# Last combination of a two-layer decoder step: normalisation moments of the odd token tiles on ScalarE, identity products and one square root at the stage's start

## The reference, cut to what matters

```python
def layer_norm(x, g, b, eps=LN_EPS):
    mu = xf.mean(-1, keepdims=True)
    var = jnp.square(xf - mu).mean(-1, keepdims=True)
    return ((xf - mu) * lax.rsqrt(var + eps) * g + b)
...
    y = y + dense_gate[:, e:e + 1] * (h @ w_down[e])
...
x = layer_norm(ALPHA * x + f, prm['ln_ffn_g'][layer], prm['ln_ffn_b'][layer])
```

## Time and profile before

| | us |
|---|---|
| median of 3 runs | 1498.75 |
| lowest, highest | 1495.86, 1498.77 |
| the profiled execution, its device time | 1502.35 |
| span of the profiled execution | 1500.5 |
| start of the last combination in it | about 1446.4 |
| end of the last VectorE instruction | about 1496.9 |
| TensorE busy, VectorE busy, ScalarE busy over the span | 92%, 49%, 29% |

### The profile page before, as it was taken

The page is one execution under the profiler, slowest core; times in us unless marked ns, Lnnn a source line. Parts: engine busy times, 40 slices in busy tenths (PEclk is TensorE's granted clock), DMA queues, the critical chain, the costliest instruction groups (busy, mean ns, idle before and its releaser), DMA issues. The chain is left out here.

```text
span 1500.5 us, 28132 instructions
## 1 busy us (share of the span) xinstructions
PE 1374.4 (92%) x11029; PEld 806.2 (54%) x11030; DVE 737.1 (49%) x1095; ACT 442.4 (29%) x804; POOL 227.3 (15%) x257
## 2 busy tenths in 40 slices
PE   6999999999689998999978999994998899999956
PEld 5666666666578886454554333331797633333322
DVE  1004444368357762677573334333795634343328
ACT  1003445542233332111113333332232133333311
POOL 4000000000333432110001111113300111111131
PEclk8999999999789998999999999997899999999978
DMA  8492000000210012100347787884503797877445
GB/s 222 85 375 91 22 29 29 29 1 0 60 37 4 4 33 78 62 29 28 122 184 294 281 309 297 328 267 141 188 1 116 269 338 262 330 285 281 155 173 208
DMA packets 73898, 226.76 MB, mean 151 GB/s; under 512 B 21970, under 2 KB 35267, under 8 KB 61226
## 3 DMA queue, kind: packets, MB, share of 16 engines
q1 hardware_dynamic: 52994, 151.13, 29.9%
q0 software_dynamic: 15184, 53.67, 10.0%
q10 hardware_dynamic: 5616, 20.45, 3.4%
HBM read 176.42 MB, written 50.35 MB: 151 GB/s over the span
## 5 line engine op out<-in xcount | busy, mean ns | idle before, releaser
L2445 PE MATMUL ex_pb<-ew_w_gate_up,ex_xT 128*64 x624 | 279.5, 601 | 5.7 <-DVE x_rows L2659 3.8
L2446 PE MATMUL ex_pb<-x_rows,ex_xT 128*64 128x512 f32 x624 | 279.5, 601 | 0.0
L517 PE MATMUL pj_pb<-pj_xT,pj_w 128*128 128x348 f32 (+1 forms) x912 | 275.5, 458 | 0.6 <-ACT pj_xT L552 0.6
L517 PEld LDWEIGHTS pj_pb<-pj_xT,pj_w 128*128 128x128 f32 x912 | 170.1, 189 | 94.5 <-issue 5.7
L2445 PEld LDWEIGHTS ex_pb<-ew_w_gate_up,ex_xT 128*64 128x64 f32 x624 | 83.0, 138 | 170.7 <-issue 170.7
L2659 DVE COPY x_rows<-ew_w_gate_up 128x2048 f32 x80 | 98.0, 1225 | 123.2 <-PE ex_pb L2446 111.7
L2430 PE MATMUL ex_pb<-ew_w_down,ex_hiddenT 128*64 x312 | 145.3, 609 | 4.7 <-ACT ex_hiddenT L2526 4.7
L2431 PE MATMUL ex_pb<-x_rows,ex_hiddenT 128*64 128x512 f32 x312 | 145.3, 609 | 0.0
L2510 ACT COPY x_rows<-ew_w_down 128x2048 f32 x39 | 74.1, 1899 | 117.5 <-PE ex_pb L2431 117.5
L2430 PEld LDWEIGHTS ex_pb<-ew_w_down,ex_hiddenT 128*64 128x64 f32 x312 | 40.3, 139 | 80.4 <-issue 80.4
L2446 PEld LDWEIGHTS ex_pb<-x_rows,ex_xT 128*64 128x64 f32 x624 | 83.0, 138 | 0.0
(11 more groups left out here) (430 smaller groups left out, 2242.7 us busy)
## 6 DMA issues: line engine op xcount, KB each, us to landing
ew_w_gate_up<-in_w_ex_gate_up SPq DMA_DIRECT2D x64, 1024.0 KB, 7.2
ew_w_down<-in_w_ex_down_by_row SPq DMA_DIRECT2D x32, 1024.0 KB, 9.2
scratch_slots_out<-ex_y_rows ACTq DMA_DIRECT2D x39, 512.0 KB
scratch_slots_out<-pj_tmp POOLq DMA_DIRECT2D x3, 4096.0 KB, 21.7
scratch_x_stored<-x_rows SPq DMA_DIRECT2D x16, 512.0 KB
pj_w<-in_w_in SPq DMA_DIRECT2D x7, 1024.0 KB, 9.3
minus_kk_then_y<-in_x_prompt SPq DMA_DIRECT2D x8, 512.0 KB, 5.5
mo_x_in<-in_x_prompt SPq DMA_DIRECT2D x8, 512.0 KB, 3.5
```

The lines of the kernel that those rows point to most:

```text
L517: last = nc.tensor.matmul(product(at)[:, 0:tn], w[:, k_slab % NW, k, c0:c0 + mrows], xT[:, k, x0:x0 + tn], start=(k == 0), stop=(k == KD - 1))
L2445: mm(pb[0:HALF, 2 + u, :], xT[:, k, 0:HALF], w[:, k, :], start=(k == 0), stop=(k == KD - 1))
L2446: last = mm(pb[HALF:P, 2 + u, :], xT[:, k, HALF:P], half_wgu[:, k, :], start=(k == 0), stop=(k == KD - 1))
```

## The change

A square root of `eps` that nobody reads (`eps_root`) is put on ScalarE after the first four diagonals. TensorE starts the stage with `keep_busy` of 28 products into bank 7, before its wait for the gathered rows of tile 0. For odd tiles (1, 3, 5, 7) ScalarE takes the moments: a pass Identity over the tile with a running sum; the sum times -1/D; a pass Square with the negated mean as bias and a running sum; and the root of the second sum over D plus eps. The results of both passes are written over `expert_rows` of that tile, and are not read. VectorE then does only centre, reciprocal and finish for odd tiles; its centre waits for the sum of squares. Even tiles are handled as before. The new helper bodies replace `norm_stats`, `norm_centre`, `norm_root` and `norm_finish` in this stage only.

```diff
+        moments = m.sb("moments", [P, 2, 5])
+        eps_root = m.sb("eps_root", [P, 1])
...
         @block.tensor
         def _(pe):
+            keep_busy(nc, pb[:, 7, :], const["ident"], 28)
             for i in range(TILES):
...
+            def moments_of(i):
+
+                n, o = rows(i), i // 2
+                seen = r[0:n, i, 0, :]
+                total, minus_mean, squares, root = (moments[0:n, o % 2, k:k + 1] for k in range(4))
+                act.wait_ge(q["res"], i + 1)
+                nc.scalar.activation(seen, summed(i), ACT.Identity, accum_out=total).then_inc(q["sum"], 1)
+                act.wait_ge(q["sum"], o + 1)
+                if o >= 2:
+                    act.wait_ge(q["g"], i - 3)
+                nc.scalar.activation(minus_mean, total, ACT.Identity, scale=-1.0 / D).then_inc(q["mean"], 1)
+                act.wait_ge(q["mean"], o + 1)
+                nc.scalar.activation(seen, summed(i), ACT.Square, bias=minus_mean, accum_out=squares).then_inc(q["squares"], 1)
+                act.wait_ge(q["squares"], o + 1)
+                if o >= 2:
+                    act.wait_ge(q["rs"], i - 3)
+                nc.scalar.activation(root, squares, ACT.Sqrt, bias=eps[0:n, :], scale=1.0 / D).then_inc(q["root"], 1)
...
             act.wait_ge(q["eps"], 1)
+            nc.scalar.activation(eps_root[:, :], eps[:, :], ACT.Sqrt)
             for i in range(TILES):
-                norm_root(nc, act, q, i, rows(i), st, eps)
+                if i % 2:
+                    moments_of(i)
+                else:
+                    root_of(i)
                 if i + 2 < TILES:
                     diagonals(i + 2)
...
             for i in range(TILES):
-                norm_stats(nc, dve, q, i, summed(i), st)
-                norm_centre(nc, dve, q, i, x_(i), summed(i), st, g)
-                norm_finish(nc, dve, q, i, x_(i), st, b)
+                n = rows(i)
+                if i % 2:
+                    shift, root, rs = (moments[0:n, i // 2 % 2, k:k + 1] for k in (1, 3, 4))
+                    dve.wait_ge(q["squares"], i // 2 + 1)
+                    stt(out=x_(i), in0=summed(i), scalar=shift, in1=g[0:n, :], op0=ALU.add, op1=ALU.mult).then_inc(q["g"], 1)
+                else:
+                    mean, root, rs = (st[0:n, i // 2 % 2, k:k + 1] for k in (12, 14, 15))
+                    stats(i)
+                    stt(out=x_(i), in0=summed(i), scalar=mean, in1=g[0:n, :], op0=ALU.subtract, op1=ALU.mult).then_inc(q["g"], 1)
```

More of the change, by code:

```diff
@@ L2698, in combine @@
         st = m.sb("stats", [P, 2, 18])
+        moments = m.sb("moments", [P, 2, 5])
+        eps_root = m.sb("eps_root", [P, 1])
         eps = m.sb("eps", [P, 1])
         pb = m.psum("pb", [P, 8, 512])
-        q = {k: m.sem(k) for k in "eps diag res st var root rs g x out".split()}
+        q = {k: m.sem(k) for k in "eps diag res st var sum mean squares root rs g x out".split()}
         s_r = [m.sem(f"rows{i}") for i in range(TILES)]
@@ L2753, in diagonals, with root_of @@
                                          scale=gates[0:n, i, c:c + 1]).then_inc(q["diag"], 1)
+            def moments_of(i):
[14 more added lines that the diff above has]
+                nc.scalar.activation(root, squares, ACT.Sqrt, bias=eps[0:n, :], scale=1.0 / D).then_inc(q["root"], 1)
+            def root_of(i):
+                n, e = rows(i), i // 2
+                act.wait_ge(q["var"], e + 1)
+                nc.scalar.activation(st[0:n, e % 2, 14:15], st[0:n, e % 2, 13:14], ACT.Sqrt, bias=eps[0:n, :]).then_inc(q["root"], 1)
             for i in range(2):
@@ L2763, in _, with stats @@
         def _(dve):
+            stt = nc.vector.scalar_tensor_tensor
             dve.wait_ge(s_ln, 32)
-            for i in range(TILES):
-                norm_stats(nc, dve, q, i, summed(i), st)
-                norm_centre(nc, dve, q, i, x_(i), summed(i), st, g)
-                norm_finish(nc, dve, q, i, x_(i), st, b)
+            def stats(i):
+                n, e = rows(i), i // 2
+                s = st[0:n, e % 2, :]
+                dve.wait_ge(q["res"], i + 1)
+                for h in range(2):
+                    last = nc.vector.bn_stats(s[:, 6 * h:6 * h + 6], summed(i)[:, 512 * h:512 * h + 512])
+                last.then_inc(q["st"], 1)
+                dve.wait_ge(q["st"], e + 1)
+                nc.vector.bn_aggr(s[:, 12:14], s[:, 0:12]).then_inc(q["var"], 1)
+                dve.wait_ge(q["var"], e + 1)
+            for i in range(TILES):
+                n = rows(i)
[7 more added lines that the diff above has]
+                    stt(out=x_(i), in0=summed(i), scalar=mean, in1=g[0:n, :], op0=ALU.subtract, op1=ALU.mult).then_inc(q["g"], 1)
+                dve.wait_ge(q["root"], i + 1)
+                nc.vector.reciprocal(rs, root).then_inc(q["rs"], 1)
+                dve.wait_ge(q["rs"], i + 1)
+                dve.wait_ge(q["g"], i + 1)
+                stt(out=x_(i), in0=x_(i), scalar=rs, in1=b[0:n, :], op0=ALU.mult, op1=ALU.add).then_inc(q["x"], 1)
 def constants():
```

## The result

| | before | after |
|---|---|---|
| median, us | 1498.77 (11 runs) | 1508.85 (11 runs) |
| lowest, highest | 1495.83, 1501.85 | 1504.56, 1516.55 |
| the profiled execution | 1502.35 | 1512.42 |
| its span | 1500.5 | 1510.6 |
| stage's start (GpSimd's first instruction in it) to tile 8's statistics | 46.27 | 58.26 |

The ratio is 1.0075, interval 1.0059 to 1.0091: about 10 us slower. The forecast was 1495.4 us, with a range of 1492.9 to 1498.6; it is missed by 13.4 us, on the wrong side, and the range doesn't hold the result.

A forecast was written before the change was run, and what follows sets the result against it. VectorE was taken to bound the last stage, TensorE the whole program. Start 1.0, table load 0.4 and statistics 6.28, less waits of 1.9 and 3 x 0.85, gave 3.3 by the chain: 1498.75 to 1495.4 us, range 1492.9 to 1498.6.

The forecast's parts named there:

- The start: Last stage's beginning: identity products let tile 0 run at full clock, so VectorE starts 1.0 us earlier.
- the line that costs the gathers and the clocks at nothing: Last stage: TensorE, gathers, stores moved up beside them and bank reads make nothing late; cost nothing.
- The products are hidden but for their end: Stage's start: TensorE awaits tile 0's rows anyhow, so identity products delay its products by only 0.5 us.
- VectorE starts 0.1 later: Tile 0: VectorE begins 0.1 us after TensorE's products end, as before, at 1457.97.
- Table load: ScalarE, tile 0: the early root moves the 1.28 us load forward, sparing VectorE's 0.39 wait; gain 0.4 us.
- Moments: ScalarE, odd tiles: Identity pass 1.02, Square pass 1.11, reads 0.20; 2.64 us until VectorE's release.
- Half of it comes: Rival, odd tiles: moments take 2.8 to 3.1 us, gain 1.5, time 1497.3 us; chance 0.17.
- ScalarE as bound: Rival, odd tiles: much slower ScalarE passes bound the stage; 1504 us at twice the pass times; chance 0.08.
- The new waits: VectorE at odd tiles waits for ScalarE's moments: 0.85 us each, 1.9 at tile 1.
- TensorE's slack of 0.4: Tile pairs: at full clock TensorE finishes 0.4 us before its products are due, staying off the chain.
- The "wrong" list: Signs against: Square over 1.5, second table load, TensorE awaited behind tile 2, or clock under 1.00 between tiles 1 and 7.
- other parts shifting: Whole program: nothing shows because other parts shift by the runs' spread of 2.9 us; chance 0.02.

The follow-up runs named there:

- e2: The kernel before plus the 28 identity products only, no moments or early root, on chip A: 1498.22 us, ratio 0.9989 to the kernel before.
- e9: The changed kernel itself, nothing altered, run again on chip C: 1497.21 us, ratio 0.9971 to the kernel before.
- e19: The changed kernel itself, nothing altered, run again on chip E: 1495.36 us, ratio 0.9979 to the kernel before.
- e6: The changed kernel without the early square root of eps, on chip B: 1511.81 us, ratio 1.0063 to the kernel before.
- e4: The changed kernel with 7 identity products of 512 columns for the 28 of 128, on chip A: 1494.40 us, ratio 0.9962 to the kernel before.
- e3: The changed kernel with 14 identity products in place of 28, on chip A: 1495.26 us, ratio 0.9966 to the kernel before.
- e11: The changed kernel with 20 identity products in place of 28, on chip C: 1494.84 us, ratio 0.9965 to the kernel before.
- e17: The changed kernel with 14 identity products in place of 28, on chip D: 1499.34 us, ratio 1.0003 to the kernel before.
- e5: The changed kernel itself, nothing altered, run again on chip B: 1511.31 us, ratio 1.0057 to the kernel before.
- e16: The changed kernel itself, nothing altered, run again on chip D: 1513.19 us, ratio 1.0092 to the kernel before.

## Why the prediction was wrong, step by step

- **The start, and with it the line that costs the gathers and the clocks at nothing: failed.** "The products are hidden but for their end" holds for the time of TensorE, and for that alone. They took 7.90 for a forecast of 7.88, and tiles 0 and 1 were done at 1459.38, 14.8 after the stage's start of 1444.58; the forecast had 1461.31, 14.9 after 1446.45. But "VectorE starts 0.1 later" is a handover, and I took its 0.1 from a stretch in which no such products stood beside the gathers. Measured: VectorE 25.44 after the start in place of 11.52. The term of +1.0 became -12.9.
- **Where it isn't held, the same term is mis-sized.** The start is worth 46.27 - 45.44 = 0.8 in e2, but the changed kernel's own products took 9.39 in e9 and 9.38 in e19, so VectorE starts at 12.98, 0.5 later than before, not 1.0 earlier. I had read the 7.88 off one row. The gain of the start needs products that end in time: 1.4 with 14 or 20 of them (11.15, 11.11).
- **Table load: right.** 0.39 gone, back in e6. The drain that the Trainium skill (ScalarE: Activation LUTs, "What ACT_TABLE_LOAD costs") adds to a load doesn't show after either: the load begins 0.02 after the diagonals' end, the root 0.01 after the load's.
- **Moments: right.** 1.00 to 1.02 and 1.11, reads of 0.19, 2.60 for 2.64. "Half of it comes" and "ScalarE as bound" are both out.
- **The new waits: right.** An odd centre comes 4.95 after its even tile's statistics (1467.44 - 1462.49 in e4), for T + 5.01; less 4.16 that is 0.79, for 0.85. The view writes 0.71, as it counts from the modelled end of the instruction ahead, 0.08 after the next could start. Tile 1: 1459.90 - 1453.92 = 5.98, so 1.82, for 1.9. Held, it is 0.71, since tile 1 has long been there.
- **TensorE's slack of 0.4: right where nothing is held,** and gone after a wait of 13 us. The "wrong" list had TensorE named behind tile 2; that is the 1.46, but by way of the clock after the hold, not of the pairs.
- **The sum.** For after: -12.93 (start) + 0.4 + 6.28 - 1.46 - 1.80 - 3 x 0.71, and 0.08 more for each of the five waits, is -12.0; measured 46.27 - 58.26 = -11.99. For e4, forecast 3.30, measured 3.36; its median is 6.3 below before. The changed kernel itself, where it isn't held, gains 46.27 - 44.16 = 2.1 of its stage (e9 and e19), for the longer products above; its medians are 2.1 and 4.0 below before.
- **The chances.** Slower had 0.10: 0.08 on ScalarE as the bound and 0.02 on other parts shifting. A cost in what the products share with the gathers had no case of its own, though it was the one thing in the change that no row of before showed beside saturated gathers (share 1.0). A bound could have been read from the rows, as a guess at the worst: the end of the gathers beside it, whose second one of tile 7 lands at 1475.75, 29.3 after the stage's start.

## What to carry to other kernels

Work on an idle engine is hidden only if its signals are too: price the handover of an engine beside saturated gathers as a cost of its own (here nothing on chips A, C and E and some 14 us on B and D), and doubt a view that names a releaser long done. An early part that fills a wait should be as short as does the job: 14 or 20 products bring up the clock as well as 28 (24 records in 10.54 us in e3 and e11, 10.46 to 10.47 in e9 and e19) and end in time, and 14 lose less where the hold is. A change whose parts can be taken alone should be tried in parts on several chips; here the moments gain 5.4 us with 14 products on chip A and 4.5 with 20 on chip C, with 14 nothing that can be measured on D, and 28 products turn the same change into a loss of 10 to 12 on B and D.

## What the runs showed of the hardware that I had not expected

- TensorE's signal can reach VectorE 14 us after its product, when identity products have run beside saturated gathers: 25.3 and 26.1 us after the stage's start for tiles done at 11.4 and 14.8. It is on two chips of the four that ran the changed kernel, and in the result's own profile, and there in every profile with 24 or 28 products. Signals between VectorE and ScalarE at that time take 0.04 us (e17).
- 28 identity products from idle take 7.8 to 8.1 us in some executions and 9.4 in others, with the same program (after 7.90, e5 8.01; e9 9.39, e16 9.40, e19 9.38).
- After 13 us of idle the granted clock was 0.50 and 0.60 in the next two stretches of back-to-back products (2.97 and 3.50 us); waits of 0.4 to 0.5 us in e4 cost nothing that shows (7.10 for sixteen records, granted clock 0.97 over 25.22 us).
- An accumulator read costs 0.19 and a pass with a running sum out of PSUM is as long as a plain copy: 1.00 to 1.02 for 1024 columns.
